# Two transformer blocks in one launch: the Hyena filter network and its taps, laid out anew in the opening

## What is computed

```python
def reference(...):
    x = first_block(...)    # pooling mixer with a modulation of c, then a SwiGLU
    return second_block(x, ...)   # MLA, conv FFN, Hyena mixer, conv FFN

def hyena_filters(length, fw1, fb1, fw2, fb2, fw3, fb3, freq, fw_out):
    t, z = hyena_positional_features(length)        # z: 512 x 33
    h = jnp.sin(freq * (z @ fw1 + fb1))             # width 64
    h = jnp.sin(freq * (h @ fw2 + fb2))
    h = jnp.sin(freq * (h @ fw3 + fb3))
    h = h @ fw_out                                  # 64 x (2 orders * 2 sides * 1024)
    ...
    return h.reshape(length, 2, 2, D_MODEL) * decay[:, None, None, :]

    z = gate * (y + d_bias[o] * z)                  # the skip of the Hyena mixer
```

## Time and profile before

| | |
|---|---|
| median of 3 runs | 1809.87 us |
| the profiled execution, span | 1812.2 us, 19372 instructions |
| PE, DVE, ACT, POOL busy | 97%, 53%, 34%, 39% |
| granted TensorE clock, mean | 0.989 |
| first product of the network | 3.61 us |
| first taps | 26.11 us |
| end of the pooling windows on TensorE | 82.0 us |
| first product after the first norm | 151.90 us |

### The profile page before, as it was taken

How to read it: one execution, slowest core, us unless ns; L and a number is a source line. 1 busy time by engine, 2 the same in 40 slices (tenths; PEclk the granted TensorE clock), 3 DMA queues, 4 the chain that set the end, 5 groups by cost and what they waited for, 6 DMA issues and landing times.

```text
span 1812.2 us, 19372 instructions
## 1 busy us (share of the span) xinstructions
PE 1750.3 (97%) x7700; PEld 1390.5 (77%) x7700; DVE 952.7 (53%) x1360; ACT 620.1 (34%) x877; POOL 699.5 (39%) x321
## 2 busy tenths in 40 slices
PE   5999999999999999999999999999999999999997
PEld 2556888888878666788888888788888788888885
DVE  7887433321265865654444213687785754444124
ACT  1524222222244554253333212532233533333122
POOL 1111444444443121434444444365553344444442
PEclk9999999999999999999999999999999999999998
DMA  9873423223222020223323222522223222332321
GB/s 338 308 287 111 133 95 103 93 94 102 95 77 67 9 70 24 81 70 99 99 93 99 99 94 93 186 94 87 88 93 114 73 93 93 102 97 93 99 98 71
DMA packets 54341, 195.60 MB, mean 108 GB/s; under 512 B 6216, under 2 KB 7176, under 8 KB 52393
## 3 DMA queue, kind: packets, MB, share of 16 engines
q1 hardware_dynamic: 52584, 188.22, 31.0%
q10 hardware_dynamic: 1666, 6.14, 1.0%
HBM read 181.75 MB, written 12.58 MB: 107 GB/s over the span
## 4 chain that ended last, share of the span: by engine, by line
PE 83%; DVE 11%; DMA 2%; POOL 2%; issue 2%; ACT 1%; SPq 0%; DVEq 0%; ACTq 0%; POOLq 0%
PE ps L514 26%; PE ps L516 26%; PE ps L515 26%; DMA mod_ring<-in_mod_t 2%; PE ps L563 1%; DVE mod_ring L1752 1%; POOL w_lo L1587 1%; DVE softmax_stats L2123 1%; DVE n_values L1932 1%; PE ps L659 1%; DVE filter_taps L1819 1%; PE ps L666 1%; DVE probs_t_lo L2175 0%; PE ps L890 0%; DVE probabilities L2129 0%
## 5 line engine op out<-in xcount | busy, mean ns | idle before, releaser
L1587 POOL TENSOR_TENSOR w_lo<-w_raw,w_hi 128x1024 fp32r<-128x1024 f32 (+1 forms) x234 | 568.8, 2432 | 825.4 <-ACT w_hi L1101 746.3
L514 PE MATMUL ps<-act_hi,w_hi 128*128 128x512 f32 x1320 | 518.0, 392 | 10.4 <-DVE act_lo L1937 3.9
L1101 ACT ACTIVATE w_hi<-w_raw 128x1024 fp32r<-128x1024 f32 (+1 forms) x238 | 251.2, 1056 | 790.4 <-PE ps L516 781.4
L515 PE MATMUL ps<-act_lo,w_hi 128*128 128x512 f32 x1320 | 514.6, 390 | 0.0
L516 PE MATMUL ps<-act_hi,w_lo 128*128 128x512 f32 x1320 | 514.4, 390 | 0.0
L514 PEld LDWEIGHTS ps<-act_hi,w_hi 128*128 128x128 f32 x1320 | 248.3, 188 | 66.2 <-DVE act_lo L1937 5.7
L516 PEld LDWEIGHTS ps<-act_hi,w_lo 128*128 128x128 f32 x1320 | 248.2, 188 | 52.3
L515 PEld LDWEIGHTS ps<-act_lo,w_hi 128*128 128x128 f32 x1320 | 248.3, 188 | 51.8 <-issue 0.7
L514 PE MATMUL ps<-f_hidden_hi,w_hi 128*128 128x512 f32 x528 | 208.2, 394 | 0.0
L516 PE MATMUL ps<-f_hidden_hi,w_lo 128*128 128x512 f32 x528 | 207.4, 393 | 0.0
L515 PE MATMUL ps<-f_hidden_lo,w_hi 128*128 128x512 f32 x528 | 205.6, 389 | 0.0
(11 more groups left out here) (291 smaller groups left out, 2316.3 us busy)
## 6 DMA issues: line engine op xcount, KB each, us to landing
w_raw<-in_w_stream SPq DMA_DIRECT2D x250, 512.0 KB, 3.5
mod_ring<-in_mod_t SPq DMA_DIRECT2D x18, 512.0 KB, 10.8
x_tokens<-in_mod_t SPq DMA_DIRECT2D x18, 512.0 KB, 9.5
spectra<-filter_spectra SPq DMA_DIRECT2D x16, 512.0 KB, 7.7
hy_filter<-spectra SPq DMA_DIRECT2D x8, 1024.0 KB, 4.8
mod_ring_more<-in_mod_t SPq DMA_DIRECT2D x12, 512.0 KB, 11.1
x_residual<-in_xT ACTq DMA_DIRECT2D x8, 256.0 KB, 10.4
x_tokens<-in_x_tokens SPq DMA_DIRECT2D x1, 2048.0 KB, 12.1
```

The lines of the kernel that those rows point to most:

```text
L514: PE.matmul(o, lh, rh, start=start, stop=False, **kw)
L515: PE.matmul(o, lh, rl, start=False, stop=False, **kw)
L1101: SC.activation(B.weights(c)[0][:, 0:n], B.WR[:, c % 2, 0:n], ACT.Copy).then_inc(S.w_hi, 1)
L1587: GP.tensor_tensor(low[:, 0:n], B.WR[:, c % 2, 0:n], f32(high[:, 0:n]), ALU.subtract).then_inc(S.w_lo, 1)
```

## The change

- The 512 times of the network are cut in two halves of 256. The first half uses partitions 0 to 63, the second 64 to 127; the three weight matrices are block diagonal (128 x 128), and come with biases and frequency in one load `network` (128 x 388). Every operation of the network is then 128 x 256 instead of 64 x 512.
- The hidden values are stored in `hidden_hi_lo`: where a half's columns are, its 64 rows hold the high part and the other 64 the low part. The output weights are stacked twice (both halves of the partitions equal), summed or subtracted, and split into `FA` (high) and `FB` (low). `taps(v)` is then two float32r passes, which give all four products of the parts.
- `fw_out` comes in two loads of 1024 KB on 128 partitions. The first serves units 0 to 3. For units 4 to 7 VectorE makes the sum of one unit at a time (`late_sum`), ScalarE its high part (`split_hi`), VectorE its low part (`split_lo`), in the midst of the units before.
- The skip is added by VectorE to the first row of the decayed taps, in units 0, 2, 4 and 6, from a row that ScalarE loads (`skip_row`).
- The waits for the network's loads ahead of ScalarE's loads go, and so do the clearing of `fw_out_sum_diff` on GpSimd and of `x_sum` on VectorE. Modulation tile 0 moves behind the network.

The diff, cut to its core (places in memory, semaphores, the removed clearing on GpSimd and the host's laying out of the inputs are left out):

```diff
--- before.py
+++ after.py
@@ -543,12 +553,16 @@
                     ins.then_inc(S.w_used, 1)
 
     def taps(v):
-        n, order, kind = unit_parts(v)
+        PE.wait_ge(S.fw_lo, split_of(v))
         for q in range(4):
             if v:
                 PE.wait_ge(S.decayed, 4 * v - 3 + q)
-            PE.matmul(ps[:, q, :], B.hidn[:, q * P:(q + 1) * P], B.fsd[:, kind, order, n * 512:(n + 1) * 512],
-                      start=True, stop=True).then_inc(S.taps, 1)
+            else:
+                PE.wait_ge(S.hid_lo, q // 2 + 1)
+            for part in (B.FA, B.FB):
+                ins = PE.matmul(ps[:, q, :], B.hid[:, q * P:(q + 1) * P], part[:, v % 4, :],
+                                start=part is B.FA, stop=part is B.FB)
+            ins.then_inc(S.taps, 1)
 
     def transform(v, parity, f):
 
...
@@ -610,18 +624,14 @@
         ins.then_inc(S.ln_mean, 1)
 
     def start():
-        PE.wait_ge(S.hy_small_in, 48)
-        PE.matmul(ps[0:HY_W, 0, :], B.fw1[:, :], B.zt[:, :], start=True, stop=True).then_inc(S.mlp, 1)
-        PE.wait_ge(S.consts_made, 6)
-        for layer in range(2):
-            PE.wait_ge(S.hid, layer + 1)
-            PE.matmul(ps[0:HY_W, 0, :], B.fws[:, layer * HY_W:(layer + 1) * HY_W], B.hidn[0:HY_W, :],
+        PE.wait_ge(S.hy_small_in, 32)
+        PE.matmul(ps[:, 0, 0:HALF], B.net[:, 0:P], B.zt[:, :], start=True, stop=True).then_inc(S.mlp, 1)
+        for layer in range(1, 3):
+            PE.wait_ge(S.hid, layer)
+            PE.matmul(ps[:, 0, 0:HALF], B.net[:, layer * P:(layer + 1) * P], B.hidn[:, :],
                       start=True, stop=True).then_inc(S.mlp, 1)
-        PE.wait_ge(S.hid, 3)
-        PE.wait_ge(S.fw_sums, 1)
-        PE.wait_ge(S.skip_in, 16)
+        PE.wait_ge(S.hid_hi, 2)
         taps(0)
-        PE.wait_ge(S.fw_sums, 2)
         taps(1)
         PE.wait_ge(S.dft_in, 16)
         unit(0)
...
@@ -1060,6 +1070,11 @@
     norm(5)
 
 
+def split_of(v):
+
+    return v % 2 + 1 if v < 4 else v - 1
+
+
 def product_slot(B, s):
 
     half, f = divmod(s, 2)
...
@@ -1101,20 +1116,35 @@
         SC.activation(B.weights(c)[0][:, 0:n], B.WR[:, c % 2, 0:n], ACT.Copy).then_inc(S.w_hi, 1)
 
     def start():
-        SC.wait_ge(S.hy_small_in, 48)
-        SC.dma_start(B.fwo, B.a["hy_fw_out"]).then_inc(S.fw_out_in, 16)
+        def skip_row(v):
+            n, order, _ = unit_parts(v)
+            if v:
+                SC.wait_ge(S.decayed, 4 * v - 7)
+            SC.dma_start(B.skip[:, :], B.a["hy_skip"][0:1, order, n * T:(n + 1) * T]).then_inc(S.skip_in, 16)
+
+        SC.dma_start(B.fwo[0][:, :, :, :], B.a["hy_fw_out"][0]).then_inc(S.fw_out_in[0], 16)
         SC.dma_start(B.decay[:, :, :], B.a["decay"][0]).then_inc(S.decay_in[0], 16)
+        skip_row(0)
         SC.dma_start(B.tab[:, :, :], B.a["dft_fwd"]).then_inc(S.dft_in, 16)
-        SC.wait_ge(S.fsd_cleared, 1)
-        SC.dma_start(B.fsd[HY_W:HY_W + 1, 0, :, :], B.a["hy_skip"]).then_inc(S.skip_in, 16)
         SC.wait_ge(S.row_in, 16)
         SC.activation(B.c_row[:, :], B.c_row[:, :], ACT.Silu).then_inc(S.silu_c, 1)
-        SC.wait_ge(S.consts_made, 6)
+
+        def split_hi(n, slots):
+            SC.wait_ge(S.fw_sums, n)
+            SC.activation(B.FA[:, slots, :], B.FS[:, slots, :], ACT.Copy).then_inc(S.fw_hi, 1)
+
         for layer in range(3):
             SC.wait_ge(S.sin_arg, layer + 1)
-            SC.activation(B.hidn[0:HY_W, :], B.flt[0:HY_W, 0, 0, :], ACT.Sin).then_inc(S.hid, 1)
+            SC.activation(B.hidn[:, :], B.flt[:, 0, 0, 0:HALF], ACT.Sin).then_inc(S.hid, 1)
+            if layer < 2:
+                split_hi(layer + 1, slice(layer, 4, 2))
+        SC.wait_ge(S.hid, 3)
+        for half in range(2):
+            rows, cols = slice(half * HY_W, (half + 1) * HY_W), slice(half * HALF, (half + 1) * HALF)
+            SC.activation(B.hid[rows, cols], B.hidn[rows, :], ACT.Copy).then_inc(S.hid_hi, 1)
         for k in range(KD):
             SC.dma_start(X[:, k, :], B.a["xT"][k * P:(k + 1) * P, :]).then_inc(S.x_in, 16)
+        SC.dma_start(B.fwo[1][:, :, :, :], B.a["hy_fw_out"][1]).then_inc(S.fw_out_in[1], 16)
         SC.dma_start(B.band[:, :, :], B.a["pool_band"]).then_inc(S.band_in, 16)
 
         def even_part(v, f):
...
@@ -1166,15 +1197,20 @@
         pool_in(4, KD)
         plus_part(2, 0)
         plus_part(2, 1)
+        skip_row(4)
+        split_hi(4, slice(1, 2))
         for k in range(KD):
             SC.activation(X[:, k, :], X[:, k, :], ACT.Copy, scale=ALPHA_1).then_inc(S.x_scaled, 1)
         copies(3)
+        split_hi(5, slice(2, 3))
         for k in range(4):
             diff_whole(k)
             diff_hi(k)
         for k in range(4, KD):
             diff_whole(k)
         copies(4)
+        skip_row(6)
+        split_hi(6, slice(3, 4))
         for k in range(4, KD):
             diff_hi(k)
         w_hi(2)
...
@@ -1792,31 +1826,54 @@
         VE.memset(B.minus_half[:, :], -0.5).then_inc(S.consts_made, 1)
         VE.memset(B.mean_w[:, :], 1.0 / D).then_inc(S.consts_made, 1)
         VE.memset(B.lead_w[:, :], 1.0 / (LEAD * P)).then_inc(S.consts_made, 1)
-        VE.memset(B.hidn[:, :], 0.0).then_inc(S.consts_made, 1)
-        VE.wait_ge(S.consts_made, 5)
-
-        VE.memset(B.hidn[HY_W:HY_W + 1, 0:1], 1.0).then_inc(S.consts_made, 1)
-        VE.wait_ge(S.hy_small_in, 48)
+        VE.wait_ge(S.hy_small_in, 32)
         for layer in range(3):
             VE.wait_ge(S.mlp, layer + 1)
-            arg = B.flt[0:HY_W, 0, 0, :]
-            at = 2 * HY_W
-            after(own.mark(VE.tensor_scalar(arg, ps[0:HY_W, 0, :], B.fws[:, at + layer:at + layer + 1],
-                                            B.fws[:, at + 3:at + 4], ALU.add, ALU.mult)))
+            arg = B.flt[:, 0, 0, 0:HALF]
+            at = 3 * P
+            after(own.mark(VE.tensor_scalar(arg, ps[:, 0, 0:HALF], B.net[:, at + layer:at + layer + 1],
+                                            B.net[:, at + 3:at + 4], ALU.add, ALU.mult)))
             reduced(arg, B.red[:, :]).then_inc(S.sin_arg, 1)
-            if layer == 0:
-                kept_rows()
-                VE.wait_ge(S.silu_c, 1)
-                mod_tiles(0, 1)
-            else:
-                VE.wait_ge(S.fw_out_in, 16)
-                VE.wait_ge(S.fsd_cleared, 1)
-                VE.tensor_tensor(B.fsd[0:HY_W, layer - 1, :, :], B.fwo[:, :, 0], B.fwo[:, :, 1],
-                                 (ALU.add, ALU.subtract)[layer - 1]).then_inc(S.fw_sums, 1)
+            if layer < 2:
+
+                VE.wait_ge(S.fw_out_in[0], 16)
+                VE.tensor_tensor(B.FS[:, layer:4:2, :], B.fwo[0][:, :, 0, :], B.fwo[0][:, :, 1, :],
+                                 (ALU.add, ALU.subtract)[layer]).then_inc(S.fw_sums, 1)
+
+        def split_lo(n, slots):
+            VE.wait_ge(S.fw_hi, n)
+            VE.tensor_tensor(B.FB[:, slots, :], B.FS[:, slots, :], f32(B.FA[:, slots, :]),
+                             ALU.subtract).then_inc(S.fw_lo, 1)
+
+        def late_sum(v):
+
+            order, kind = unit_parts(v)[1:]
+            VE.wait_ge(S.fw_out_in[1], 16)
+            VE.wait_ge(S.taps, 4 * (v - 4) + 4)
+            VE.tensor_tensor(B.FS[:, v % 4, :], B.fwo[1][:, order, 0, :], B.fwo[1][:, order, 1, :],
+                             (ALU.add, ALU.subtract)[kind]).then_inc(S.fw_sums, 1)
+
+        split_lo(1, slice(0, 4, 2))
+        for half in range(2):
+            rows, cols = slice(half * HY_W, (half + 1) * HY_W), slice(half * HALF, (half + 1) * HALF)
+            VE.wait_ge(S.hid_hi, half + 1)
+            VE.tensor_tensor(B.hid[(1 - half) * HY_W:(2 - half) * HY_W, cols], B.hidn[rows, :], f32(B.hid[rows, cols]),
+                             ALU.subtract).then_inc(S.hid_lo, 1)
+        split_lo(2, slice(1, 4, 2))
+        kept_rows()
+        VE.wait_ge(S.silu_c, 1)
+        mod_tiles(0, 1)
 
         def decay_tile(v, q):
             VE.wait_ge(S.taps, 4 * v + q + 1)
-            VE.tensor_tensor(B.flt[:, v % 2, q, :], ps[:, q, :], B.decay[:, q, :], ALU.mult).then_inc(S.decayed, 1)
+            ins = VE.tensor_tensor(B.flt[:, v % 2, q, :], ps[:, q, :], B.decay[:, q, :], ALU.mult)
+            if q == 0 and v % 2 == 0:
+
+                after(own.mark(ins))
+                row = B.flt[0:1, 0, 0, :]
+                VE.wait_ge(S.skip_in, 16 * (v // 2 + 1))
+                ins = VE.tensor_tensor(row, row, B.skip[:, :], ALU.add)
+            ins.then_inc(S.decayed, 1)
 
         def decays(v):
             VE.wait_ge(S.decay_in[v // 4], 16)
...
@@ -1860,19 +1917,26 @@
         decays(1)
         mod_tiles(5, 9)
         butterfly(0)
+        late_sum(4)
         mod_tiles(9, 11)
         decays(2)
         mod_tiles(11, 15)
+        split_lo(3, slice(0, 1))
+        late_sum(5)
         butterfly(1)
         mod_tiles(15, 16)
         decays(3)
+        late_sum(6)
         mod_tiles(16, 20)
+        split_lo(4, slice(1, 2))
         butterfly(2)
         decays(4)
+        late_sum(7)
         mod_tiles(20, 21)
```

(4 more changed lines are left out.)

59 lines of the change are left out of this document (41 added, 18 removed).

## The result

| | kernel before | changed kernel |
|---|---|---|
| first set, median | 1810.36 us (4 runs) | 1827.24 us (4 runs, 1823.77 to 1827.91) |
| ratio, 95% interval | | 1.0086 [1.0074, 1.0097] |
| second set, median | 1810.9 us (12 runs) | 1824.74 us (5 runs, 1824.48 to 1827.21) |
| ratio, 95% interval | | 1.0080 [1.0067, 1.0092] |
| profiled execution, span | 1812.2 us | 1822.5 us |

The forecast was 1812.9 us, range 1806 to 1817. It missed by 12 to 14 us. The sets of the changed kernel have four and five runs and overlap, so what an experiment takes off is given against both.

A forecast was written before the change was run, and what follows sets the result against it. It took TensorE, VectorE, ScalarE and the DMA queues as level, with VectorE setting the opening's end. An earlier first decay and added VectorE and ScalarE work summed to +3.0: 1809.9 + 3.0 = 1812.9 us, range 1806 to 1817.

The forecast's parts named there:

- The tail: VectorE, pooled tiles to centring: added low parts and a skip, some 1.5 us vanishing in waits; +0.4 us left.
- the opening's +3.0: Whole opening: centring starts at 135 instead of 132.05, all behind it as it was; sum +3.0 us.
- the way from there to the even part of unit 3: ScalarE's 11.8 us get a skip-row issue (0.45) and a high part (0.55): 12.8; even part at 71.8, +2.4.
- The clock: Unit 2: TensorE waits some 6 us for its even part, then runs partly at 1.2 GHz: +0.2 us (0 to 1.7).
- The start: Filter network beside ScalarE's loads: first product at 6.5 us (4.0 to 8.3), first sine at 12.3 instead of 10.10.
- D: Start of the first decay on VectorE: 26.4 us instead of 28.32, bounds 22.8 and 28.7.
- the third case: Slower rival: network's loads and row of c come last, Silu ahead of first sine; D 28.7, +5.3, 1815.2 us; chance 0.28.
- One packet from each in turn: Loads at the start: a DMA engine alternates packets between two queues, so the first network product begins by 8.3 us.
- From D to `affine`: First decay to `affine`: 28.4 us before; new skips, sums and low part on VectorE ahead of `affine`, 3.3 us.
- The faster rival: TensorE bounds after all, VectorE's and ScalarE's additions find room: 1809.9 - 11.5 = 1798.4 us; chance 0.10.

The follow-up runs named there:

- the repaired kernel: Changed kernel whole with first loads held, idle TensorE filled at four places and both of GpSimd's low parts moved: 1816.30 us, ratio 1.0030.
- All three at once: Changed kernel with idle TensorE filled, no skip adds, and no late sums and splits: excess 4.5 us over the kernel before, ratio 1.0017.

## Why the prediction was wrong

- **The tail, "+0.4", is the step that failed**: it was +7.3 (from +6.1 to +13.4 in the table), 6.9 of the 10.4 us by which the opening's +3.0 fell short of the +13.4; the other 3.5 are the start (1.9), the way to `affine` (1.1) and the way from there to the even part of unit 3 (0.5). Its parts in the trace: low part ahead of the pooled tiles 0.6; half clock of 12 products behind the 5.11 us wait 0.9 more than before; low part and skip add 1.3; half clock of 12 products behind the new 2.81 us wait 2.5; the collision at 142.76 2.0. The prediction let 1.5 us vanish in VectorE's waits because taps(6) are shorter. In truth shorter taps made TensorE come early, wait and slow down, and VectorE's waits for products grew to 8.3 us from 4.8. The collision it had not looked for.
- **The clock, "+0.2 (0 to 1.7)"**, was sized from one stretch at 0.80. In unit 2 it was 2.6 us (6.25 for eight records, where 16 took 7.03). That TensorE idles some 6 us there was right (5.76); that its price is hidden "since ScalarE's list runs beside it" was wrong in part, since the plus parts that ScalarE copies, the high part behind them and the low part on VectorE all wait for the slow products. Of the 2.6 us 1.15 reached ScalarE's list, as its wait for the second plus part, which starts at 70.38. The issue of a skip row, put at 0.45, cost it nothing, so from the first `pool_in` to the even part of unit 3 it was 13.5 us where the forecast has 13.0. The even part came at +6.1, not +2.4. The larger price of the clock is in the tail.
- **The start**: the mechanism (ScalarE's rows delay the network's, the row of c comes ahead of the first sine) was right, its size was not: the network at 9.13 lies beyond the bound of 8.3, the first sine at 14.22, and D was 28.30, near the value of the third case (28.7) and not 26.4. It cost 1.9 us of the miss. "One packet from each in turn" fits the counts from 5 us on, but not the stretch from 4 to 5 us, in which SyncE's queue moved none; what held it there no run shows. By the rule of the Trainium skill that was weighed, *DMA: Bandwidth & Descriptors*, section on queues, rings and completion order (whole packets of about 9 to 17 descriptors), the network would have begun near 5.7. The start at 9.13 speaks against that estimate; the counts do not decide on the rule, as the prediction says, since they are summed over 16 engines.
- **From D to `affine`**: 32.5 forecast, 33.6 measured. The blocked add (2.34 for 2.4) was right. By the rule of the Trainium skill, *SBUF — State Buffer*, "Who interferes with whom", VectorE's instruction with two inputs waits for GpSimd's; the trace agrees, the add ends 0.5 us after the `w_lo` that began 0.56 us ahead of it. That one partition waits as 128 do is shown by this trace. The 1.1 us are the butterflies of unit 0, which waited 1.2 us for a unit 0 at half clock in part (8.29 us for 16 records, 7.03 before).
- **The sum was made against one profiled execution**, some 3.6 us above the median of its kind. Profile against profile the loss is 10.3 us, median against median 13.8 and 16.9: such a difference is as large as the whole forecast. It is not an error of a step but a bound on what such a sum can say.
- The faster rival, TensorE as the bound, is refuted from both sides: the change that took 12.8 us from TensorE made the kernel slower, giving them back (one pass) and even adding products that nobody reads made it faster.

What stays open: 3.0 us of excess between the two sets of the changed kernel, and the 5.4 us that the repaired kernel still lacks though its opening ends as early as before in the traces (149.76 and 149.51 for the first scaled tile). Its profiled run was the fastest of eight and the one before a slow one, which accounts for the gap between the profiles (0.6 us) and the medians. All three at once, profiled in the slowest of its eleven runs, ends the opening at 149.12 and yet has a span of 1814.0: there the loss lies behind the opening, with the clock below 0.95 near 1130, 1230 and 1280 us where the kernel before has 1280 and 1420. Whether that is chance or comes with the changed opening, one trace of each does not tell.

## What to carry to other kernels

Busy time near 100% on one engine does not make it the bound when another engine's list sets when it may go on. Price a saving by the wait that takes its place, and add the products behind that wait at half clock. Work moved from a matrix engine with room to a vector engine on the path can cost more than its own length (here 5.4 us for 4.4). Where a wait of several us can't be removed, products that nobody reads, sized to end a little before the wait does, are worth trying; and an idle third engine is not free to take over work if it reads the same memory.

## What the runs showed of the hardware that was not expected

- After waits as short as 2.81 us the granted clock fell to the 1.2 GHz level for most of the next 12 products (0.43 us a product in place of 0.23); after waits of 2.1 us, in the kernels without skip adds and without late parts, some eight of them were slow. With 0.66 us left of the wait it stayed at 1.00.
- A VectorE operation of 128x8 with one input in memory took 2.21 us (0.17 alone) beside GpSimd's `w_lo`: not only those with two inputs are blocked.
- The blocking is mutual: two GpSimd sums of 512 columns took 5.66 us where 1.27 each is their time alone.
- Between two queues the bytes followed packet size: 2.96 MB and 0.82 MB in the same 12 us, for 395 and 408 packets.
- The granted clock of a profile can miss half clock near the start: the second trace of the changed kernel has 1.00 in 34:44, where unit 0 took 8.10 us for 7.03.
